# Sums of the first two column tiles shared by VectorE and TensorE, low parts ahead of shift and scale, earlier zeroing, and a new spread of the second layer's sums

## The chip, the cores and the metric

One core of a Trainium2 chip runs the whole program in one launch. The metric is the device time in microseconds (us), as the median of three runs. The names of the engines are those of the profile: PE is TensorE, DVE is VectorE, ACT is ScalarE, POOL is GpSimd, SP is SyncE, which only issues transfers here.

## The reference

256 tokens of width 1024 pass through two layers of a modulated block (retention, then a softmax attention with forget gates) and a second block (window attention, a gated linear recurrence and a feed-forward part). Everything is float32. What matters here is the start and the retention layer:

```python
c_act = jax.nn.silu(c)                                   # (1, 1024)
for i in range(DEPTH):                                   # DEPTH = 2
    shift, scale, gate = jnp.split(c_act @ mod_w[i] + mod_b[i], 3, axis=-1)   # mod_w[i]: 1024 x 3072
    h = _rms_norm(x, norm_g[i]) * (1.0 + scale[:, None, :]) + shift[:, None, :]
    y = _retention(h, ...)  if i == 0 else  _forgetting_attention(h, ...)
    x = x + gate[:, None, :] * y

# _retention: q, k, v, g = split(h @ w_in)  (1024 x 6144); rope on q, k; decayed scores; o = scores @ v
    o = _layer_norm(_from_chunks(o)).reshape(b, s, RET_DV)
    return (o.astype(h.dtype) * jax.nn.silu(g)) @ w_out  # w_out: 2048 x 1024
```

The product `c_act @ mod_w` is a vector by a matrix, so it costs the reading of the matrix (12 MB a layer) and little arithmetic on PE.

## The kernel before

**Products.** A product of float32 matrices is made of three products in a reduced format: each operand is split into a high part and a low part (`whi`, `wlo` for weights, `ahi`, `alo` for the left side), and PE adds high x high, high x low and low x high (L353 to L355 in `products`, L438 to L440 in `rows_unit`). Weights come in units of 512 KB (128 partitions x 1024 columns). For each unit SP issues the load into one of 8 raw buffers, ACT copies it to `whi` (L1754), DVE subtracts to get `wlo` (L995), and PE runs 12 products of 128x512. `ring_to(u)` on ACT and on DVE does this work for all items up to unit u. There are 3 buffers for the split parts, so ACT can split unit v only when PE has finished unit v-3.

**Item order.** `weight_stream` writes one list of items: weight units ("w") and "mod" items, each 128 rows of `mod_w` (1024 columns). SP loads them in list order, 8 in flight, and DVE works them off in list order, each raising the semaphore `used`. A mod item costs DVE one multiply-and-add of 128x1024 into `acc` (L1004 in the profile, a helper's line); it costs ACT and PE nothing.

**The first stage (units 0 to 11).** The normalised input is transposed per column tile k of 128 (`turn_x0`), then ACT applies shift and scale (`x0_high`) and makes the high part, DVE the low part (`x0_low`). Shift and scale of layer 0 are needed per column tile before anything can be multiplied: the columns of `mod_w[0]` for tiles (0), (1), (2,3), (4,5), (6,7), the groups g = 0 to 4, are loaded by SP between the first units (`load_mod`), 1 MB for each tile. DVE adds up rows 0 to 6 of eight, each weighted with a column of silu(c), into `macc` (`mod_sums`). PE multiplies row 7 directly and adds the sum over partitions of `macc` with a product of one column against ones (`shift_scale`, L421 and L423), DVE adds bias and gain (`modulated(k)`), ACT and DVE make the parts of the left side, and PE can run the units of this tile. Units 3j and 3j+1 belong to tiles 2j and 2j+1 (`rows_unit`), unit 3j+2 to both (`products`).

**Retention (units 12 to 47).** In each chunk of four units PE makes 512 columns of the projection. After each of the first four chunks DVE applies rope to two banks. From unit 28 on, `weigh(h)` computes a head, DVE takes mean and variance (`weighed`), normalises two 128x512 tiles from PSUM (L1001) and multiplies with silu(g) (`gated`). Layer 1's mod items and layer 0's gate items are spread over units 12 to 55. `after_ss` sums layer 1's `acc` over partitions on PE. Units 48 to 63 are the output projection.

**What sets the order.** Each engine's program is written out by hand in order of execution. Nothing is planned by a cost table, apart from the item list.

## Time and profile before

| | us |
|---|---|
| median of 3 runs | 745.84 (745.13 to 746.02) |
| the profiled execution | 745.61 |
| its span in the trace | 743.8 |
| PE busy | 712.3 (96%) |
| DVE busy | 508.4 (68%) |
| ACT busy | 379.3 (51%) |
| granted TensorE clock, mean | 0.986 of full |

The span runs from the first instruction to the last; 1.8 us of the execution lie around it. Busy shares are means over very different stages: over the first 16.7 us PE mostly waits, in most later stages it has no gap. A granted clock of 0.50 is the lower of TensorE's two levels (1.2 GHz), 1.00 the upper one (2.4 GHz). A float32 product appears twice in a row of the timeline ("x2" for one written instruction).

### The profile page before, as it was taken

How to read it: one execution, taken by the hardware profiler on the slowest of the kernel's cores; microseconds unless marked ns; L12 is line 12 of the kernel's file. 1: busy time of each engine (PE TensorE's matmuls, PEld its weight loads, DVE VectorE, ACT ScalarE, POOL GpSimd, SP SyncE). 2: the span in 40 equal slices, each digit the busy share in tenths (PEclk: the TensorE clock that was granted, in tenths of full speed). 3: DMA queues.
4: the chain of work that ended last, by engine and by line, in shares of the span. 5: the costliest groups of instructions: out<-in, count | busy, mean ns of one | idle time of the engine just before them, and what ended most of it. 6: DMA issues, size and time to landing. Idle time of an engine off the chain costs nothing.

```text
span 743.8 us, 9342 instructions
## 1 busy us (share of the span) xinstructions
PE 712.3 (96%) x3520; PEld 585.5 (79%) x3520; DVE 508.4 (68%) x731; ACT 379.3 (51%) x559; POOL 22.2 (3%) x36
## 2 busy tenths in 40 slices
PE   5899999999999899999999899999999999999996
PEld 4777777778778678878888788888887888888884
DVE  4787998796865867845577779966676465555444
ACT  5337543454544647663645664454566544444343
POOL 4100000000000000000001100000000000000000
PEclk8799999999999999999999999999999999999998
DMA  9997766657784357753245453343466556655511
GB/s 297 370 336 259 259 238 214 226 182 248 230 274 145 94 193 251 233 164 95 97 151 173 153 172 95 119 136 122 133 199 195 176 170 198 194 182 183 194 66 57
DMA packets 74476, 138.95 MB, mean 187 GB/s; under 512 B 5748, under 2 KB 18272, under 8 KB 74432
## 3 DMA queue, kind: packets, MB, share of 16 engines
q1 hardware_dynamic: 72816, 134.82, 55.4%
q0 software_dynamic: 880, 1.64, 0.7%
q10 hardware_dynamic: 736, 1.90, 0.7%
q8 instruction: 28, 0.46, 0.3%
q14 instruction: 16, 0.13, 0.1%
HBM read 137.30 MB, written 1.05 MB: 186 GB/s over the span
## 4 chain that ended last, share of the span: by engine, by line
PE 84%; DVE 9%; issue 3%; ACT 2%; DMA 1%; SPq 0%; DVEq 0%; ACTq 0%
PE G L353 22%; PE G L355 22%; PE G L354 22%; PE T L374 4%; DVE arena L995 2%; DVE wlo L995 2%; PE T L820 2%; PE T L693 1%; PE T L674 1%; PE G L438 1%; DMA arena<-in_mod_w_dram 1%; DVE arena L1004 1%; PE G L440 1%; PE G L439 1%; PE T L729 1%
## 5 line engine op out<-in xcount | busy, mean ns | idle before, releaser
L995 DVE TENSOR_TENSOR wlo<-raw,whi 128x1024 fp32r<-128x1024 f32 x206 | 251.2, 1223 | 137.9 <-ACT whi L1754 137.0
L353 PE MATMUL G<-whi,ahi 128*128 128x512 f32 x776 | 314.2, 405 | 6.0 <-DVE wlo L995 5.4
L355 PE MATMUL G<-whi,alo 128*128 128x512 f32 x776 | 303.9, 392 | 0.0
L354 PE MATMUL G<-wlo,ahi 128*128 128x512 f32 x776 | 303.2, 391 | 0.0
L1754 ACT ACTIVATE whi<-raw 128x1024 fp32r<-128x1024 f32 x206 | 217.2, 1059 | 131.2 <-PE G L355 118.1
L353 PEld LDWEIGHTS G<-whi,ahi 128*128 128x128 f32 x776 | 146.2, 188 | 38.8 <-DVE wlo L995 8.6
L355 PEld LDWEIGHTS G<-whi,alo 128*128 128x128 f32 x776 | 146.0, 188 | 31.8
L354 PEld LDWEIGHTS G<-wlo,ahi 128*128 128x128 f32 x776 | 146.4, 189 | 29.3 <-issue 1.4
L1756 ACT ACTIVATE arena<-T,st 128x128 f32<-128x128 f32 (+1 forms) x48 | 16.7, 422 | 39.8 <-DVE st L1372 39.8
L1754 ACT ACTIVATE ahi<-T 128x512 fp32r<-128x512 f32 x25 | 15.0, 599 | 42.3 <-PE T L374 42.3
L1756 ACT ACT_TABLE_LOAD x27 | 34.6, 1283 | 2.3 <-issue 1.8
L374 PE MATMUL T<-head,arena 128*128 128x128 f32 x212 | 32.5, 277 | 2.4 <-ACT arena L1756 0.9
L374 PEld LDWEIGHTS T<-head,arena 128*128 128x128 f32 x212 | 25.8, 144 | 9.1 <-ACT arena L1756 1.3
L995 DVE TENSOR_TENSOR alo<-T,ahi 128x512 fp32r<-128x512 f32 x25 | 17.3, 690 | 21.3 <-ACT ahi L1754 21.3
L1004 DVE SCALAR_TENSOR_TENSOR acc<-raw,cact,acc 128x1024 f32<-128x1024 f32 x24 | 30.7, 1281 | 1.6 <-DVE wlo L995 0.5
L995 DVE TENSOR_TENSOR arena<-arena 128x512 f32<-128x512 f32 (+7 forms) x46 | 23.0, 551 | 1.2 <-ACT arena L1756 0.9
L1004 DVE SCALAR_TENSOR_TENSOR arena<-arena,cact 128x512 f32<-128x512 f32 (+1 forms) x30 | 19.3, 645 | 1.0
L1756 ACT ACTIVATE st<-st 128x1 f32<-128x1 f32 (+3 forms) x21 | 4.3, 205 | 30.7 <-DVE st L999 18.8
L1372 DVE TENSOR_REDUCE st<-T 128x2 f32<-128x512 f32 (+1 forms) x18 | 12.3, 689 | 11.0 <-PE T L676 5.9
L438 PE MATMUL G<-whi,ahi 128*128 128x512 f32 x32 | 14.6, 455 | 5.2 <-DVE alo L995 3.1
L820 PEld LDWEIGHTS T<-arena 128*128 128x128 f32 x128 | 15.4, 191 | 0.9 <-DVE arena L995 0.4
L1754 ACT ACTIVATE arena<-T 128x512 f32<-128x512 f32 x11 | 6.5, 596 | 18.6 <-PE T L374 16.0
(212 smaller groups left out, 610.5 us busy)
## 6 DMA issues: line engine op xcount, KB each, us to landing
raw<-in_ret_w_in_dram SPq DMA_DIRECT2D x48, 512.0 KB, 5.3
raw<-in_w_gate_up_dram SPq DMA_DIRECT2D x40, 512.0 KB, 4.0
raw<-in_mod_w_dram SPq DMA_DIRECT2D x32, 512.0 KB, 5.2
raw<-in_fox_w_in_dram SPq DMA_DIRECT2D x32, 512.0 KB, 4.8
raw<-in_w_in_dram SPq DMA_DIRECT2D x28, 512.0 KB, 3.5
raw<-in_w_down_dram SPq DMA_DIRECT2D x22, 512.0 KB, 4.5
arena<-in_mod_w_dram SPq DMA_DIRECT2D x16, 512.0 KB, 8.7
raw<-in_ret_w_out_dram SPq DMA_DIRECT2D x16, 512.0 KB, 5.5
```

Source lines behind the costliest of these rows:

```text
L353: e.matmul(o, ah, wh, start=first and k == 0, stop=False)
L354: e.matmul(o, ah, wl, start=False, stop=False)
L355: done = e.matmul(o, al, wh, start=False, stop=last and k == 1)
L374: d = e.transpose(t[:, n * P:(n + 1) * P], s, idf)
L438: e.matmul(o, ah, wh, start=k == 0, stop=False)
L439: e.matmul(o, ah, wl, start=False, stop=False)
L820: d = e.matmul(t[:, h * P:(h + 1) * P], k[:, h, m * P:(m + 1) * P], q[:, h, m * P:(m + 1) * P], start=True, stop=True)
L995: e.tensor_tensor(o, a, b, op).then_inc(sig[name], 1)
L1004: e.scalar_tensor_tensor(out=o, in0=a, scalar=s, in1=b, op0=op0, op1=op1).then_inc(sig[name], 1)
L1372: e.tensor_reduce(st[:, 44 + 4 * r:44 + 4 * r + n], t[:, :].rearrange("p (h n) -> p h n", h=n), AX.X, ALU.max, negate=True).then_inc(sig[f ...
L1754: d = e.activation(o, a, f, scale=scale)
L1756: d = e.activation(o, a, f, scale=scale, bias=bias)
```

## The change

1. **Sums shared (groups 0 and 1).** `VECTOR_ROWS` gives DVE rows 0 to 3 for the first two groups and leaves rows 4 to 7 to PE (`own_rows`), which makes eight products of one column for a tile where it made two. The other groups stay at seven rows on DVE. The sums of tile 0 go to banks G, those of tile 1 to T[0] and T[1].
2. **Order on PE at the start.** 20 idle transposes instead of 24, then the own rows of tile 0, the transposes of the small rows and of both tiles (`turn_rows`), the rest of the sums, 6 idle transposes, the first half of unit 0 (columns 0 to 511), the sums of tile 1, the second half of unit 0.
3. **Low parts first.** In the first stage DVE makes `wlo` of unit 3j before `modulated` of its tiles; ACT splits one unit more before the left sides.
4. **Zeroing.** POOL clears `acc` (128x3072) right after its small row loads, where it waited for `used` >= 2.
5. **Table.** ACT no longer loads the square-root table ahead of the two squares.
6. **Angles.** The three pieces of the rope angles are made together behind `wlo` of unit 12.
7. **Retention.** The normalisation of a head moves from DVE to ACT (`normalise`: scale and bias from two columns), `gated` comes later.
8. **Spread of mod items.** The distances are given by a table; five items now come with units 12 to 15, fewer from unit 16 to 28, and again many from unit 44 on. `after_ss` moves from units 41 to 44 to units 52 to 55.

```diff
-    for j in range(24):
-        after.setdefault(j * 15 // 8, []).append(mods[j])
+    after = (-1, 0, 1, 2, 3, 6, 9, 13, 16, 18, 20, 23, 25, 27, 30, 32, 34, 35, 36, 38, 39, 40, 41, 42)
+VECTOR_ROWS = [4, 4, 7, 7, 7]
@@ PE
-            for _ in range(24):
-                e.transpose(G[2][:, 0:P], idf, idf)
+            keep_warm(20)
+            def own_rows(g, i, a):
+                r0 = VECTOR_ROWS[g]
+                for r in range(r0, 8):
+                    e.matmul(sums_of(SUMMED[g][i], a), mod_tile(g)[:, a, r, i * P:(i + 1) * P], cact[:, r:r + 1], start=r == r0, stop=False)
+            def other_rows(g, i, a):
+                on_.wait_ge(sig["macc"], g + 1)
+                return e.matmul(sums_of(SUMMED[g][i], a), macc[:, g % 2, a, i * P:(i + 1) * P], ones[:, 0:1], start=False, stop=True)
-            turn_x0(0)
-            shift_scale(0)
-            turn_x0(1)
-            rows_unit(0, 0)
-            shift_scale(1)
+            first_sums(0, turn_rows)
+            keep_warm(6)
+            rows_unit(0, 0, (0,))
             on_.wait_ge(sig["rows_read"], 3)
+            first_sums(1)
+            rows_unit(0, 0, (1,))
-                    if u + 2 in (43, 44, 45, 46):
-                        after_ss(u + 2 - 43)
+                if 4 <= n < 8:
+                    after_ss(n - 4)
@@ DVE
-            mod_sums(0, 0, 2)
             on_.wait_ge(sig["rms_act"], 1)
             e.reciprocal(st[:, 0:2], st[:, 0:2]).then_inc(sig["rms"], 1)
-            mod_sums(0, 2, 7)
+            mod_sums(0, 0, 4)
...
-            mod_sums(1, 0, 7)
...
+            mod_sums(1, 0, 4)
+            ring_to(1)
             modulated(1)
-            ring_to(1)
+            ring_to(2)
             x0_low(1)
             for g in (2, 3, 4):
                 k, u = 2 * g - 2, 3 * g - 3
                 mod_sums(g, 0, 4)
-                if g > 2:
-                    ring_to(u - 1)
+                ring_to(u - 1)
                 mod_sums(g, 4, 7)
+                ring_to(u)
                 modulated(k)
                 modulated(k + 1)
-                ring_to(u)
                 x0_low(k)
...
             u = 12
+            ring_to(u)
+            for part in range(3):
+                angles(part)
...
-                    on_.wait_ge(sig["left_turned"], 2 * h - 2)
-                    ts(on[:, h % 2, m, :], t[:, :], mv[:, 0:1], mv[:, 1:2], ALU.subtract, ALU.mult, "weigh_dve")
+                    stt(st[:, 2 + m:3 + m], mv[:, 0:1], -1.0, mv[:, 1:2], ALU.mult, ALU.mult, "weigh_dve")
-            chunk_of([[(weighed, 0), (gated, 0)], [], [], [(scored, 2)]])
-            chunk_of([[(scored, 3)], [(weighed, 1), (gated, 1)], [(left_low, 8)], [(left_low, 10)]])
+            chunk_of([[(weighed, 0)], [], [(gated, 0)], [(scored, 2)]])
+            chunk_of([[(scored, 3)], [(weighed, 1)], [(left_low, 8)], [(left_low, 10), (gated, 1)]])
@@ ACT
-            sqrt_table()
-            ring_to(1)
+            ring_to(2)
             x0_high(1)
-            ring_to(2)
-            ring_to(3)
-            x0_high(2)
-            x0_high(3)
-            ring_to(5)
-            for k in (4, 6):
+            for k in (2, 4, 6):
                 ring_to(3 * k // 2 + 1)
+            def normalise(h):
+                for m in range(2):
+                    on_.wait_ge(sig["weigh_dve"], 10 * h + 8 + 2 * m)
+                    on_.wait_ge(sig["left_turned"], 2 * h - 2)
+                    act(on[:, h % 2, m, :], T[bank_of["weigh", h, m]][:, :], ACT.Identity, "normed",
+                        scale=st[:, 21 + 2 * m:22 + 2 * m], bias=st[:, 2 + m:3 + m])
@@ POOL
+            fill(acc[:, :], 0.0, "acc_zero")
 ...
-            on_.wait_ge(sig["used"], 2)
-            fill(acc[:, :], 0.0, "acc_zero")
```

On PE, the start of the program before stands in a row as follows (`head` are the constants with the identity, `cact` is silu(c), `arena` holds the rows of `mod_w` and the normalised input; three rows make one sixth of the first unit's products):

```order
L383 MATMUL G<-head 128x128 x24
L387 MATMUL T<-head,rows 128x128
L374 MATMUL T<-head,arena 128x128 x2
L421 MATMUL T<-cact,arena 128x1
L423 MATMUL T<-ones,arena 128x1
L421 MATMUL T<-cact,arena 128x1
L423 MATMUL T<-ones,arena 128x1
L374 MATMUL T<-head,arena 128x128 x2
L438 MATMUL G<-whi,ahi 128x512
L439 MATMUL G<-wlo,ahi 128x512
L440 MATMUL G<-whi,alo 128x512
```

In the changed kernel, the same place on PE:

```order
L387 MATMUL G<-head 128x128 x20
L422 MATMUL G<-cact,arena 128x1 x8
L482 MATMUL T<-head,rows 128x128
L381 MATMUL T<-head,arena 128x128 x4
L427 MATMUL G<-ones,arena 128x1 x2
L387 MATMUL G<-head 128x128 x6
L471 MATMUL G<-whi,ahi 128x512
L472 MATMUL G<-wlo,ahi 128x512
L473 MATMUL G<-whi,alo 128x512
```

The products with `cact` grow from two to eight and stand ahead of the transposes; after one more triple like the last three rows, the eight and two products of tile 1 follow, where they stood behind all four triples.

On DVE, the second group of sums before, up to the low part of tile 2's left side (`AB` holds shift and scale):

```order
L999 TENSOR_SCALAR arena<-arena,cact 128x512
L1004 SCALAR_TENSOR_TENSOR arena<-arena,cact 128x512 x6
L995 TENSOR_TENSOR AB<-T,mbc 128x1
L1001 TENSOR_SCALAR AB<-T,mb,cols 128x1
L995 TENSOR_TENSOR AB<-T,mbc 128x1
L1001 TENSOR_SCALAR AB<-T,mb,cols 128x1
L995 TENSOR_TENSOR wlo<-raw,whi 128x1024
L995 TENSOR_TENSOR alo<-gate,ahi 128x256
```

The same place on DVE in the changed kernel:

```order
L1040 TENSOR_SCALAR arena<-arena,cact 128x512
L1045 SCALAR_TENSOR_TENSOR arena<-arena,cact 128x512 x6
L1036 TENSOR_TENSOR wlo<-raw,whi 128x1024
L1036 TENSOR_TENSOR AB<-T,mbc 128x1
L1042 TENSOR_SCALAR AB<-T,mb,cols 128x1
L1036 TENSOR_TENSOR AB<-T,mbc 128x1
L1042 TENSOR_SCALAR AB<-T,mb,cols 128x1
L1036 TENSOR_TENSOR alo<-gate,ahi 128x256
```

The low part of unit 3 has moved ahead of shift and scale; the same holds for units 6 and 9 in the next groups.

## Rows read from the trace of the kernel before

**Rows 1.** The page: busy time of the engines; `wlo` subtractions; mod items on DVE.
```profile
PE 712.3 (96%) x3520; PEld 585.5 (79%) x3520; DVE 508.4 (68%) x731; ACT 379.3 (51%) x559; POOL 22.2 (3%) x36
...
L995 DVE TENSOR_TENSOR wlo<-raw,whi 128x1024 fp32r<-128x1024 f32 x206 | 251.2, 1223 | 137.9 <-ACT whi L1754 137.0
...
L1004 DVE SCALAR_TENSOR_TENSOR acc<-raw,cact,acc 128x1024 f32<-128x1024 f32 x24 | 30.7, 1281 | 1.6 <-DVE wlo L995 0.5
```
**Rows 2.** Windows, PE: stretch, length, busy us (count), granted clock, DMA share, GB/s.
```profile
10.00:16.70 6.70, 2.87 (x14) 0.71 1.12 325
22.00:24.00 2.00, 0.04 (x1) 0.77 1.08 376
24.00:29.00 5.00, 5.00 (x12) 0.50 1.05 378
34.00:52.00 18.00, 16.53 (x81) 1.00 1.06 381
80.00:140.00 60.00, 56.46 (x261) 1.00 0.67 230
```
**Rows 3.** Timeline, 5 to 17 us: start, duration, instruction, [idle before <- releaser].
```profile
5.43 1.28 ACT L1756 ACT_TABLE_LOAD   x1
...
6.83 1.04 ACT L1752 ACTIVATE arena<-x 128x1024 f32<-128x1024 f32 x1
...
9.24 0.20 ACT L1756 ACTIVATE st<-st 128x2 f32<-128x2 f32 x1 [0.24 <-DVE st L1001]
9.65 0.35 DVE L999 TENSOR_SCALAR arena<-arena,cact 128x256 f32<-128x256 f32 x1 [0.44 <-DMA arena<-in_mod_w_dram]
...
10.55 2.57 DVE L1004 SCALAR_TENSOR_TENSOR arena<-arena,cact 128x256 f32<-128x256 f32 x5
...
11.11 0.30 PE L387 MATMUL T<-head,rows 128*128 128x128 f32 x1 [1.06 <-DMA rows<-in_fox_k_gain_dram]
...
13.18 0.58 PE L423 MATMUL T<-ones,arena 128*128 128x1 f32 x2 [0.60 <-DVE arena L1004]
...
14.05 0.57 PE L423 MATMUL T<-ones,arena 128*128 128x1 f32 x2
...
16.71 0.77 PE L438 MATMUL G<-whi,ahi 128*128 128x512 f32 x1 [1.57 <-DVE alo L995]
```
**Rows 4.** Timeline, 25 to 36 us: group 2's sums, unit 3's split, unit 3's start.
```profile
25.55 0.83 DVE L999 TENSOR_SCALAR arena<-arena,cact 128x512 f32<-128x512 f32 x1
...
26.08 1.06 ACT L1754 ACTIVATE whi<-raw 128x1024 fp32r<-128x1024 f32 x1 [1.77 <-DMA raw<-in_ret_w_in_dram]
...
26.42 4.76 DVE L1004 SCALAR_TENSOR_TENSOR arena<-arena,cact 128x512 f32<-128x512 f32 x6
...
31.52 0.36 PE L423 MATMUL T<-ones,arena 128*128 128x1 f32 x2
...
32.86 0.36 PE L423 MATMUL T<-ones,arena 128*128 128x1 f32 x2
...
35.22 0.47 PE L438 MATMUL G<-whi,ahi 128*128 128x512 f32 x1 [0.52 <-DVE alo L995]
```
**Rows 5.** Timeline, PE: first product of unit 6, last of unit 7, first of unit 9.
```profile
47.25 0.47 PE L438 MATMUL G<-whi,ahi 128*128 128x512 f32 x1 [0.50 <-DVE alo L995]
...
52.59 0.39 PE L440 MATMUL G<-whi,alo 128*128 128x512 f32 x1
...
58.48 0.47 PE L438 MATMUL G<-whi,ahi 128*128 128x512 f32 x1 [0.52 <-DVE alo L995]
```
**Rows 6.** Timeline, 73 to 133 us: angles, rope's wait, normalisation, a wait for `wlo`.
```profile
73.32 1.34 DVE L1004 SCALAR_TENSOR_TENSOR arena<-arena 128x256 f32<-128x256 f32 x3
...
81.37 0.66 PE L374 MATMUL T<-head,arena 128*128 128x128 f32 x4 [0.84 <-DVE arena L995]
...
126.94 0.81 DVE L1001 TENSOR_SCALAR arena<-T,st 128x512 f32<-128x512 f32 x1
...
132.25 0.50 PE L353 MATMUL G<-whi,ahi 128*128 128x512 f32 x1 [1.56 <-DVE wlo L995]
```

More of the change, by code:

```diff
@@ L116, in weight_stream @@
     mods = [mod(1, k, c0) for k in range(8) for c0 in (0, D)] + [mod(0, k, 2 * D) for k in range(8)]
-    after = {}
-    for j in range(24):
-        after.setdefault(j * 15 // 8, []).append(mods[j])
-    for n, u in enumerate(main):
-        out += [u, *after.get(n, [])]
+    after = (-1, 0, 1, 2, 3, 6, 9, 13, 16, 18, 20, 23, 25, 27, 30, 32, 34, 35, 36, 38, 39, 40, 41, 42)
+    for n in range(-1, len(main)):
+        if n >= 0:
+            out.append(main[n])
+        out += [mods[j] for j in range(24) if after[j] == n]
     fox = [u for c in range(8) for u in chunk(W1, 512 * c)]
@@ L375, in transposes, with keep_warm @@
                 d.then_inc(sig[name], 1)
+            def keep_warm(n):
+                for _ in range(n):
+                    e.transpose(G[2][:, 0:P], idf, idf)
             on_.wait_ge(sig["c_in"], 16)
@@ L417, in shift_scale, with summed, first_sums, rows_unit @@
                     on_.wait_ge(sig[f"mod_in{i}"], n)
+            def summed(k):
+                for m in range(2):
+                    ready[k, m] = (sig["x0"], k + 1)
+            def first_sums(g, between=None):
+                mod_landed(g)
+                for a in range(2):
+                    own_rows(g, 0, a)
+                if between is not None:
+                    between()
+                for a in range(2):
+                    d = other_rows(g, 0, a)
+                d.then_inc(sig["sums"], 1)
+                summed(g)
+            def shift_scale(g):
+                mod_landed(g)
                 for i, k in enumerate(SUMMED[g]):
                     for a in range(2):
-                        o = T[2 + k % 2][:, 256 + a:257 + a]
-                        e.matmul(o, raw0[:, a, 7, i * P:(i + 1) * P], cact[:, 7:8], start=True, stop=False)
-                        on_.wait_ge(sig["macc"], g + 1)
-                        d = e.matmul(o, sums[:, a, i * P:(i + 1) * P], ones[:, 0:1], start=False, stop=True)
+                        own_rows(g, i, a)
+                        d = other_rows(g, i, a)
                     d.then_inc(sig["sums"], 1)
-                    for m in range(2):
-                        ready[k, m] = (sig["x0"], k + 1)
-            def rows_unit(u, k):
+                    summed(k)
+            def rows_unit(u, k, columns=(0, 1)):
                 on_.wait_ge(sig["used"], item_of[u] + 1)
@@ L432, in rows_unit @@
                 j = u % NH
-                for c in range(2):
+                for c in columns:
                     wh, wl = whi[:, j, c * 512:(c + 1) * 512], wlo[:, j, c * 512:(c + 1) * 512]
@@ L443, in rows_unit, with turn_rows @@
                     done_at[u, c] = products_n[0]
-            turn_x0(0)
-            shift_scale(0)
-            turn_x0(1)
-            rows_unit(0, 0)
-            shift_scale(1)
+            def turn_rows():
+                on_.wait_ge(sig["filled"], 1)
+                on_.wait_ge(sig["rows_in"], 16 * 9)
+                t = bank("rows", sig["rows_read"], 3)
+                e.transpose(t[:, 0:P], rows[:, :], idf).then_inc(sig["rows_turned"], 1)
+                turn_x0(0)
+                turn_x0(1)
+            first_sums(0, turn_rows)
+            keep_warm(6)
+            rows_unit(0, 0, (0,))
             on_.wait_ge(sig["rows_read"], 3)
+            first_sums(1)
+            rows_unit(0, 0, (1,))
             for k in range(0, 8, 2):
@@ L1187, in _ @@
                     u += 1
-                    if c == 0 and k < 3:
-                        angles(k)
-                    elif c == 3 and k >= 2:
+                    if c == 3 and k >= 2:
                         scored(k - 2)
@@ L1240, in chunk_of @@
                 for k in range(4):
-                    if u + 2 == 46:
-                        after_ss()
                     ring_to(u + 2)
@@ L1272, in _ @@
             for n in range(12):
+                if n == 8:
+                    after_ss()
                 ring_to(u + 2)
```

44 lines of the change are left out of this document (20 added, 24 removed).

## The prediction

> **What bounds the kernel now.** I read the page first. PE is busy for 712.3 of 743.8 us [rows 1], so no work is to be saved: the change has to fill gaps of PE, or to keep its clock up. The table of windows says where they lie [rows 2]. From 10 to 16.7 us PE is busy for 2.87 of 6.70 us, and the granted clock sinks to 0.71 in the mean. From 22 to 24 PE stands still, and from 24 to 29 it runs at 0.50, the lower level, where twelve products take the whole 5 us. From 34 to 52 it lacks 1.5 us, with the clock at 1.00. From 80 to 140 it lacks 60.00 - 56.46 = 3.5 us. One more thing is in these rows: up to 52 us the DMA share stays above 1 and 325 to 381 GB/s flow, so in the first stage transfers land when they land, whatever the engines do.
>
> The timeline then shows each gap's last wait. At the start the chain runs through DVE's seven rows of group 0, the sums on PE, shift and scale, ACT and the low part, and unit 0 starts at 16.71 [rows 3]. Unit 3 starts at 35.22 behind the low part of its left side; unit 6 at 47.25 and unit 9 at 58.48 likewise [rows 4, 5]. In retention PE waits for rope (0.84 at 81.37) and once 1.56 for a `wlo` that stands on DVE behind normalisation, gate and a mod item [rows 6].
>
> **The start.** Group 0 lands at 9.65 in both kernels [rows 3]. Five additions took 2.57, 0.51 each, so four rows end at 9.65 + 0.35 + 3 x 0.51 = 11.5 on DVE, where seven ended at 13.18. PE's new products: at full clock six steps of this kind take 32.86 - 31.52 = 1.34, 0.22 each [rows 4]; at the lower one two take 14.05 - 13.18, 0.44 each [rows 3]. Eight own products from 9.65 end at 11.4 (13.2 at the lower clock). The small rows come at 11.11 and are not moved. One transpose of 0.30, four short ones (0.6 together), two products of 0.22: the sums of tile 0 are there at about 12.8, before at 14.05 + 0.44 = 14.5. Behind them runs the same chain, 16.71 - 14.5 = 2.2. Unit 0 starts at 15.0, 1.7 earlier. The six idle transposes lie in this chain's wait.
>
> Dropping the early table load costs nothing on this path: the load of 1.28 at 5.43 stood ahead of the first square (6.83); now the two squares, 1.04 each, come first and the load follows at about 7.6. The root is then possible at about 9, at 9.24 before [rows 3]. For this price there is a rule that speaks against the change. In rows 3 a square follows the load's end within 0.12 us, and the load starts at 5.43, at the end of the instruction before. The Trainium skill (ScalarE: Activation LUTs, What ACT_TABLE_LOAD costs) adds a drain of about 1.4 us to each load; by it the root would come 1.4 later and unit 0 up to as much, at 16.4 instead of 15.0. The trace does not bear the drain out.
>
> Zeroing `acc` earlier takes POOL out of DVE's way: one scaling of 128x512 took 0.83 at 25.55 [rows 4]. Half of that at most is won, and it isn't late there any more. The other end is a loss of as much if POOL's small loads came later; nothing waits for those in this stage. I take 0.
>
> **Units 0 to 2 and the start of unit 3.** From 15.0: six products of 0.23 (52.59 - 47.25 = 5.34 for 23 steps [rows 5]) to 16.4, ten short ones of tile 1 to 18.6 (19.4 if their rows or the first half come later), six products to 20.9, and unit 1 from about 21.8, where shift, scale and the low part of unit 2 (1.22 [rows 1]) stand ahead of it. Before, it came behind 23 us and ran at the lower clock. If the clock is low for part of this, some six to ten products at +0.2 each, unit 1 ends between 24.5 and 26. Four transposes and half of unit 2 add 2.0, the eight sums of group 2 add 1.8: they end at 28.3 to 29.8.
>
> Here the moved low part counts. Unit 3's raw data land at 26.08, ACT needs 1.06 [rows 4] and DVE 1.22, so shift and scale of tile 2 cannot be made before 28.4. Behind them stand 2.1 for AB, ACT and the low part (the chain above). Unit 3 starts at 30.6, at 35.22 before: **4.6 gained**. Faster work upstream gives no more; this landing is the floor. Before, the same low part stood behind shift and scale and delayed the left side's.
>
> **Groups 3 and 4.** 36 products of 0.232 are 8.35, four transposes 0.6, eight sums 1.8: 10.75 of work for PE. Before, a group took 47.25 - 35.22 = 12.0 and then 58.48 - 47.25 = 11.2. With `wlo` out of the chain sums, shift and scale, left side, 0.3 of waiting remains, and I take 11.0: unit 9 at 52.6 instead of 58.48, **1.3 more, 5.9 together**. The landings allow it: unit 6's data are 3.7 MB behind unit 3's, 9.6 us at 381 GB/s, so at 35.7, and are wanted at about 38.
>
> **Units 12 to 15.** Unit 12 starts at 52.6 + 8.35 = 61.0. On DVE `wlo` of unit 12 ends at about 58.0; behind it now stand three pieces of angles (1.34 for one [rows 6], 4.0), a mod item (1.28 [rows 1]) and `wlo` of unit 13 (1.22): 64.5. PE wants it at 61.0 + 2.8 = 63.8. **0.7 lost.** From then on each unit brings 1.28 + 1.22 = 2.5 on DVE against 2.8 on PE. The five items are the price paid for fewer later.
>
> **Units 16 to 47.** Rope then starts when PE is done with its banks, not 1.5 later; in each chunk DVE loses a mod item of 1.28 or two, and in the stretch of 132.25 two normalisations (0.81 each) for two tiny instructions, and the two products with the gate step back behind two `wlo`. All 3.5 of idle time should go but for 0.2 in each of two chunks, where one mod item still stands between rope and `wlo`: **3.1 gained**. The normalisation costs ACT something the trace doesn't show in this form; between 0.2 (its two-column root [rows 3]) and 1.06 (a full split), and I take 0.8, DVE's for the same tile. ACT is busy for 51% and sits behind PE's buffers; were it on the path, eight of them would cost 6.4.
>
> **Late items and the rest.** From unit 44 to 55 nearly every unit has a mod item: 2.5 against 2.8, with buffers for two units as cover; 0 taken. `after_ss` is the same 16 products of 0.22 at another place: 0.
>
> **Sum.** 5.9 - 0.7 + 3.1 = 8.3. The profiled execution took 745.6 (span 743.8 and 1.8 around it), 0.2 under the median of the runs. Forecast: 745.6 - 8.3 = **737.3 us**.
>
> **The rivals.**
> *The clock stays down through units 0 to 2.* It fell in the stretch of 10 to 16.7 and again after 22 [rows 2], both times behind short products and a wait; the new start has twenty one-column products, ten of them between the halves of unit 0. The Trainium skill (TensorE: Matmul & The Clock Gate, Part 1) says the lower clock is the default and activity lifts it; the rows agree. For it to last, the six idle transposes would have to be too few. Then the ten short ones take 4.4, unit 1 ends at 29, and unit 3 starts at 34.2: 1.0 gained instead of 4.6, **740.9**.
> *DVE becomes the bound where items are dense.* Units 12 to 15 ask it for four `wlo`, five items and the angles, 4.9 + 6.4 + 4.0 = 15.3, against 11.1 on PE. If its lead is used up by then, 4.2 are lost instead of 0.7: **740.8**. For it: DVE is full from 80 on before. Against it: it waited 137.9 us for `whi`, so it usually has a lead [rows 1].
> *The low parts tie each group to its landing.* If units 6 and 9 land 2 later than I count, unit 9 starts 2 later: **739.3**. Against it: 381 GB/s is a mean of 18 us.
> *Slower: the clock is low as far as unit 5.* A product takes 0.42 then (5.00 for 12 [rows 2]), 0.2 more. Before, about 18 ran so; now it would be 72 of six units, 54 x 0.2 = 10.8 more, against the 8.3 gained: **748**. It decides from 42 more such products on (8.3 / 0.2). Between 34 and 52 PE stood still for 1.5 in sum and kept 1.00 [rows 2], which speaks against it.
> *The change doesn't do what it says*: DVE's additions weren't the last wait at the start but the small rows at 11.11; then 0.5 of the 1.7 goes, hidden by the floor at 26.08 anyway.
>
> **How the numbers follow.** The forecast, 0.62, with a range of its own of 735.3 to 739.3; clock 0.13; dense items 0.12; landings 0.07; slower 0.05, the rest (0.01) near no change. Range for 8 in 10: 735.0 to 741.5, which takes in the clock's and the items' cases and leaves out the slower one and a gain of over 10. A measurement of this kernel tells 0.2% (1.5 us) from no change. Faster 0.92, same 0.03, slower 0.05.
>
> **What would show it.** Unit 0's first product near 15.0, unit 3's near 30.6 behind a `whi` released by its raw data near 26.1; unit 9 near 52.6; granted clock 1.00 from 24 to 29; a wait for `wlo` under 1 us near 64; PE idle under 0.6 in the 60 us from unit 16 on; no wait at unit 31. The forecast is wrong if unit 3 starts after 32, if the clock shows 0.50 beyond 24, or if PE waits for `wlo` more than 2 us in units 12 to 16.

## Result and profile after

| us | before | after |
|---|---|---|
| median | 745.49 (744.32 to 746.02, 6 runs) | 739.07 (735.23 to 741.07, 6 runs) |
| profiled execution | 745.61 | 737.51 |
| its span | 743.8 | 735.7 |
| granted clock, mean | 0.986 | 0.997 |

The ratio is 0.9912, 95% interval 0.9884 to 0.994. The medians are 6.4 us apart, the two profiled executions 8.1. The changed kernel scatters by 5.8 us where the kernel before scatters by 1.7. That scatter turns out to be the main thing to explain.

The page of the changed kernel, the row of the engines, beside [rows 1]:

```profile
PE 712.5 (97%) x3546; PEld 587.4 (80%) x3546; DVE 502.0 (68%) x725; ACT 384.1 (52%) x566; POOL 22.1 (3%) x36
```

PE's work is what it was (712.5 against 712.3). What went is its idle time. The windows of PE after the change (stretch, length, busy us and count, granted clock, DMA share, GB/s) answer to [rows 2]:

```profile
10.00:16.70 6.70, 6.68 (x31) 1.00 1.12 320
16.70:20.00 3.30, 2.60 (x6) 1.00 1.08 352
24.00:29.00 5.00, 4.40 (x22) 1.00 1.06 381
34.00:52.00 18.00, 18.00 (x98) 1.00 1.06 381
80.00:140.00 60.00, 59.46 (x272) 1.00 0.63 211
```

From 34 to 52 no idle time is left, and from 80 to 140 it is 0.54, where 3.54 stood. From 24 to 29 there are 22 products, where twelve ran at 0.50. The first two rows deceive, though. They say 1.00, but PE is busy for 6.68 of 6.70 us and unit 0 still starts late. The timeline of the start shows why (start, duration, instruction, idle before and releaser), beside [rows 3]:

```profile
5.24 4.53 PE L387 MATMUL G<-head 128*128 128x128 f32 x20
...
5.97 2.68 POOL L2297 MEMSET acc<- 128x3072 f32 x1
...
7.61 1.28 ACT L1794 ACT_TABLE_LOAD   x1
7.62 1.05 DVE L1042 TENSOR_SCALAR st<-st 128x2 f32<-128x2 f32 x1 [7.62 <-ACT arena L1790]
...
8.90 0.20 ACT L1794 ACTIVATE st<-st 128x2 f32<-128x2 f32 x1
...
9.94 3.55 PE L422 MATMUL G<-cact,arena 128*128 128x1 f32 x16 [0.18 <-DMA arena<-in_mod_w_dram]
...
10.38 1.53 DVE L1045 SCALAR_TENSOR_TENSOR arena<-arena,cact 128x256 f32<-128x256 f32 x3
...
15.16 1.52 PE L387 MATMUL G<-head 128*128 128x128 f32 x6
...
17.40 0.77 PE L471 MATMUL G<-whi,ahi 128*128 128x512 f32 x1 [0.72 <-DVE alo L1036]
17.96 0.63 PE L472 MATMUL G<-wlo,ahi 128*128 128x512 f32 x1
18.39 0.63 PE L473 MATMUL G<-whi,alo 128*128 128x512 f32 x1
...
20.10 2.28 PE L422 MATMUL T<-cact,arena 128*128 128x1 f32 x16
```

Eight own products (16 entries) take 3.55 us, 0.44 each, and the six idle transposes 1.52, 0.25 each. The six products of unit 0 stand 0.43 apart, as the twelve at a granted 0.50 did (5.00 / 12 = 0.42, [rows 2]). So PE ran at the lower level from its start to about 21 us, whatever the windows say. The trace's own record of the clock begins only at 21.0 us, with the upper level, and a window counts time without a record as 1.00. DVE had its four rows done at 11.9; PE was the late one. From 20.10 the eight own products of tile 1 take only 2.28: within them the clock rises.

The starts of the units, each from its first product in the timelines, give the ledger of the whole gain:

| first product of | before | after | gained so far | forecast |
|---|---|---|---|---|
| unit 0 | 16.71 | 17.40 | -0.7 | +1.7 |
| unit 3 | 35.22 | 33.08 | 2.1 | 4.6 |
| unit 9 | 58.48 | 54.19 | 4.3 | 5.9 |
| unit 12 | 66.77 | 62.43 | 4.3 | 5.9 |
| unit 16 | 77.65 | 74.53 | 3.1 | 5.2 |
| unit 30 | 127.25 | 122.45 | 4.8 | |
| unit 31 | 132.25 | 125.65 | 6.6 | 8.3 |
| unit 100 | 397.53 | 391.10 | 6.4 | 8.3 |
| unit 110 | 430.76 | 422.73 | 8.0 | 8.3 |
| end | 743.8 | 735.7 | 8.1 | 8.3 |

The last step of 1.6 lies far from anything the change touches. In the kernel before PE waits twice for the residual there (timeline):

```profile
413.12 0.66 PE L374 MATMUL T<-head,x 128*128 128x128 f32 x4 [0.69 <-DVE x L995]
...
415.02 0.66 PE L374 MATMUL T<-head,x 128*128 128x128 f32 x4 [1.24 <-DVE x L995]
```

A window of PE in the same trace shows the clock lower behind them:

```profile
416.00:420.00 4.00, 4.00 (x13) 0.62 0.42 131
```

In the changed kernel the same two waits stand there (0.69 and 1.23 us), and the clock stayed up. Over the fourteen profiles of this study (both kernels and twelve variants) the stretch from unit 100 to unit 110 takes either 31.6 us (ten of them) or 33.2 (before, e3, e7, e12); the one from unit 110 to the end takes 312.9 to 313.1 in all. So 1.6 us of the profiled gain is this fall of the clock, which comes behind the same waits in some executions and not in others. Without it the gain is 6.4 in the profile, as it is between the medians.

### The profile page after: what moved, and what is told of

It reads as the page before. It is cut to its first block, busy times and chain, and to the rows that moved or that the text cites. A ratio compares the mean times of both kernels' runs of the same rounds, so it can differ in the third digit from the quotient of the medians.

```text
span 735.7 us, 9394 instructions
## 1 busy us (share of the span) xinstructions
PE 712.5 (97%) x3546; PEld 587.4 (80%) x3546; DVE 502.0 (68%) x725; ACT 384.1 (52%) x566; POOL 22.1 (3%) x36
## 3 DMA queue, kind: packets, MB, share of 16 engines
HBM read 137.30 MB, written 1.05 MB: 188 GB/s over the span
## 4 chain that ended last, share of the span: by engine, by line
PE 88%; DVE 7%; ACT 2%; issue 2%; DMA 1%; SPq 0%; DVEq 0%; ACTq 0%
PE G L360 23%; PE G L362 22%; PE G L361 22%; PE T L381 4%; PE T L861 2%; DVE wlo L1036 2%; PE T L734 1%; PE T L715 1%; DVE arena L1036 1%; DMA arena<-in_mod_w_dram 1%; DVE arena L1045 1%; PE G L471 1%; PE G L472 1%; PE G L473 1%; PE T L770 1%
## 5 line engine op out<-in xcount | busy, mean ns | idle before, releaser
L360 PE MATMUL G<-whi,ahi 128*128 128x512 f32 x776 | 314.0, 405 | 4.7 <-DVE wlo L1036 4.2
L1794 ACT ACTIVATE arena<-T,st 128x128 f32<-128x128 f32 (+2 forms) x56 | 22.4, 471 | 39.8 <-DVE st L1410 39.8
L1410 DVE TENSOR_REDUCE st<-T 128x2 f32<-128x512 f32 (+1 forms) x18 | 12.3, 689 | 11.0 <-PE T L717 5.9
L1045 DVE SCALAR_TENSOR_TENSOR arena<-arena,cact 128x512 f32<-128x512 f32 (+1 forms) x24 | 16.4, 685 | 0.9
L1792 ACT ACTIVATE arena<-arena 128x512 f32<-128x512 f32 x14 | 8.3, 639 | 14.4 <-DVE arena L1036 14.4
L861 PE MATMUL T<-arena 128*128 128x128 f32 x128 | 15.7, 275 | 0.0
```

Source lines behind the costliest of these rows:

```text
L360: e.matmul(o, ah, wh, start=first and k == 0, stop=False)
L861: d = e.matmul(t[:, h * P:(h + 1) * P], k[:, h, m * P:(m + 1) * P], q[:, h, m * P:(m + 1) * P], start=True, stop=True)
L1045: e.scalar_tensor_tensor(out=o, in0=a, scalar=s, in1=b, op0=op0, op1=op1).then_inc(sig[name], 1)
L1410: e.tensor_reduce(st[:, 44 + 4 * r:44 + 4 * r + n], t[:, :].rearrange("p (h n) -> p h n", h=n), AX.X, ALU.max, negate=True).then_inc(sig[f ...
L1792: d = e.activation(o, a, f, scale=scale)
L1794: d = e.activation(o, a, f, scale=scale, bias=bias)
```

## Experiments

Unless something else is said, each kernel is the changed one with the edit shown; "u3" is the start of unit 3's first product. Three groups ran (e1 to e4, e5 to e8, e9 to e12), each beside its own 11 runs of the kernel before, with medians 745.94, 745.17 and 745.37. The 95% interval of every variant's ratio overlaps that of the changed kernel (0.9884 to 0.994), so the medians alone separate none of them from it. What an edit does is read from the distances in the profiled executions, one for each kernel.

### e1: all seven rows of every group on DVE

```diff
-VECTOR_ROWS = [4, 4, 7, 7, 7]
+VECTOR_ROWS = [7, 7, 7, 7, 7]
-            mod_sums(0, 0, 4)
+            mod_sums(0, 0, 7)
-            mod_sums(1, 0, 4)
+            mod_sums(1, 0, 7)
```

> The changed kernel with one thing undone: DVE adds up seven rows again in groups 0 and 1 too, PE multiplies only row 7 itself; the order on PE stays. Theory A (sharing the sums takes work off the chain, as predicted): the sums of tile 0 come later, macc at about 13.5 instead of 11.9, unit 0 starts about 1 later than the 17.4 of the changed kernel, unit 3 0.5 to 1 later, time +0.5 to +1. Theory B (the own products run at the lower clock, 3.55 us for eight, so they are the last wait at the start themselves and sharing gives nothing): unit 0 starts at 16.4 to 17.2, unit 3 within 0.5 of 33.1, time within 0.5 of the changed kernel's 739.

Measured 736.61 (735.54 to 738.55, 5 runs), ratio 0.9891 [0.9874, 0.9908]; u0 16.64, u3 31.86, u31 124.17. PE in the timeline of e1:

```profile
9.91 0.98 PE L422 MATMUL G<-cact,arena 128*128 128x1 f32 x4 [0.15 <-DMA arena<-in_mod_w_dram]
...
13.53 1.01 PE L427 MATMUL G<-ones,arena 128*128 128x1 f32 x4 [1.47 <-DVE arena L1045]
...
16.64 0.76 PE L471 MATMUL G<-whi,ahi 128*128 128x512 f32 x1 [0.72 <-DVE alo L1036]
```

The clock is at its lower level here too (0.98 for two products; the record begins at 24.5 us), but PE has only two of them and waits 1.47 us for DVE. Unit 0 starts 0.8 earlier than with shared sums, as theory B had it, and unit 3 1.2 earlier, which neither theory had. The sharing, meant to shorten the start, lengthened it in the profiled execution of the changed kernel.

### e2: low parts of units 3, 6 and 9 behind shift and scale again

```diff
-                ring_to(u)
                 modulated(k)
                 modulated(k + 1)
+                ring_to(u)
```

> The changed kernel with one thing undone: the low part of units 3, 6 and 9 stands behind shift and scale again. If the moved low parts give what the prediction said, each of the three starts is 0.4 to 0.8 later: unit 9 at 55.5 to 56.5 instead of 54.19, time +1.5 to +2. If the landing of the raw data binds there (rival), units 3, 6 and 9 start as before or earlier: +0.

Measured 740.79 (739.36 to 741.81, 6 runs), ratio 0.9937 [0.9923, 0.9951]. Unit 0 started at 15.02 in this execution, so only the distances tell: unit 3 to unit 6 and unit 6 to unit 9 take 11.24 and 11.23, against 10.56 and 10.55 with the low parts first. PE waits again in each group:

```profile
45.47 0.48 PE L471 MATMUL G<-whi,ahi 128*128 128x512 f32 x1 [0.48 <-DVE alo L1036]
...
56.70 0.48 PE L471 MATMUL G<-whi,ahi 128*128 128x512 f32 x1 [0.48 <-DVE alo L1036]
```

The order is worth 0.7 us in each of groups 3 and 4. If it is worth as much in group 2, which this execution can't show, that makes about 2, near the 1.7 between the medians.

### e3: mod items spread evenly, as before

```diff
-    after = (-1, 0, 1, 2, 3, 6, 9, 13, 16, 18, ...)
+    after = (0, 1, 3, 5, 7, 9, 11, 13, 15, 16, ...)
```

> The changed kernel with the old distances of the mod items (none ahead of unit 12, every second unit). Theory: the waits in units 16 to 31 come back in part, +1.7 at units 17 and 18 and up to +0.5 at unit 31, while the 1.2 lost at units 13 and 14 is won back: net +0.5 to +1.5. Rival (the normalisation alone removed the waits): net -1.2.

Measured 739.88 (738.02 to 740.28, 5 runs), ratio 0.992 [0.9906, 0.9934]. From unit 12 to unit 31 this kernel takes 63.88 us, the changed one 63.22, the one before 65.48. One wait is back in retention, at unit 18:

```profile
81.89 0.50 PE L360 MATMUL G<-whi,ahi 128*128 128x512 f32 x1 [0.59 <-DVE wlo L1036]
```

The spread is worth 0.7 us, inside the theory's range, but of the 1.2 lost in units 12 to 15 only 0.2 comes back (unit 12 to unit 16 takes 11.91 us here, 12.10 in the changed kernel, 10.88 before). Most of the gain in retention is not the spread's doing, nor is most of that loss.

### e4 and e10: 26 idle transposes at the start instead of 20

```diff
-            keep_warm(20)
+            keep_warm(26)
```

> The changed kernel with 26 idle transposes at the start instead of 20. Theory (clock): the transposes of the changed kernel stand 0.22 apart, which is the lower level, and PE's clock rises only at about 20 us; with six more the clock has risen before the own products, which then take 1.8 instead of 3.55: unit 0 at 15.5 to 16.3 instead of 17.4, unit 3 about 1 earlier, time -0.5 to -1.5, and less scatter between runs. Rival (the six stand in the way): the own products start 0.5 to 1 later, at the same low rate, and everything is that much later, time +0.5 to +1.

Measured 735.39 (734.82 to 738.08, 4 runs), ratio 0.9873 [0.9855, 0.989]. PE in the timeline of e4:

```profile
9.90 1.92 PE L422 MATMUL G<-cact,arena 128*128 128x1 f32 x16 [0.26 <-DMA arena<-in_mod_w_dram]
...
12.62 0.85 PE L387 MATMUL G<-head 128*128 128x128 f32 x6
14.86 0.76 PE L471 MATMUL G<-whi,ahi 128*128 128x512 f32 x1 [1.39 <-DVE alo L1036]
```

The theory's cause came, with more effect than it expected (15.5 at best for unit 0). The own products take 1.92 instead of 3.55. Unit 0 starts at 14.86 (forecast 15.0), unit 3 at 30.44 (30.6), unit 9 at 51.74 (52.6). What binds unit 3 here are DVE's own items one behind the other: the last sum of group 2 ends at 27.33 and `wlo`, released by nothing, runs from 27.25. The raw data were there at 25.35:

```profile
25.01 2.33 DVE L1045 SCALAR_TENSOR_TENSOR arena<-arena,cact 128x512 f32<-128x512 f32 x3
25.35 1.06 ACT L1792 ACTIVATE whi<-raw 128x1024 fp32r<-128x1024 f32 x1 [3.67 <-DMA raw<-in_ret_w_in_dram]
...
27.25 1.22 DVE L1036 TENSOR_TENSOR wlo<-raw,whi 128x1024 fp32r<-128x1024 f32 x1
```

The same kernel ran a second time, as e10:

> The changed kernel with 26 idle transposes instead of 20, a second time, on another chip job: is it a version that beats both kernels by more than its own scatter? Theory (the six transposes bridge the wait for group 0, so that the own products run at the upper level): 735.4, between 734.8 and 738.1, unit 0 at about 14.9 and unit 3 at about 30.4. Rival (four runs happened to fall well; the clock's moment is luck whatever the count): a median near the changed kernel's, 738 to 739, with a scatter of 4 us or more, and unit 0 at 15.6 or later.

Measured 735.72 (735.35 to 739.79, 5 runs), ratio 0.9884 [0.9865, 0.9903]; u0 14.65, u3 31.18. Seven of the nine runs of e4 and e10 lie below 737, of the six of the changed kernel one. By its medians it is the fastest version of the study, about 10 us below the kernel before. Against the changed kernel the intervals still overlap, and e11 (735.94) and e1 (736.61) can't be told from it.

### e5: normalisation on DVE again, everything else as changed

```diff
+                    ts(on[:, h % 2, m, :], T[bank_of["weigh", h, m]][:, :], mv[:, 0:1], mv[:, 1:2], ALU.subtract, ALU.mult, "normed")
...
-                    act(on[:, h % 2, m, :], T[bank_of["weigh", h, m]][:, :], ACT.Identity, "normed",
-                        scale=st[:, 21 + 2 * m:22 + 2 * m], bias=st[:, 2 + m:3 + m])
```

> The changed kernel with the normalisation of the heads back on DVE (two scalings of 128x512 a head, 0.81 each, beside the tiny instructions; gated stays in its later place). Theory of the prediction: the wait of unit 31 (1.56 before, gone after) was removed by taking 1.6 of work off DVE and by the later gate; undone, 0 to 0.6 of it comes back, because the gate (1.28) still stands behind: time +0 to +0.6. Rival (the ACT version is what counts): the whole 1.8 between units 30 and 31 comes back. Rival (it costs ACT, and ACT was on the path): time falls by up to 0.8 elsewhere in units 28 to 47.

Measured 739.23 (737.8 to 739.51, 4 runs), ratio 0.9916 [0.9903, 0.993]. From unit 30 to unit 31 it takes 3.92 us, against 3.20 in the changed kernel and 5.00 before. DVE and PE in its timeline, from the second of the two normalisations on:

```profile
121.61 0.80 DVE L1042 TENSOR_SCALAR arena<-T,st 128x512 f32<-128x512 f32 x1
122.33 1.27 DVE L1045 SCALAR_TENSOR_TENSOR acc<-raw,cact,acc 128x1024 f32<-128x1024 f32 x1
123.53 2.35 DVE L1036 TENSOR_TENSOR wlo<-raw,whi 128x1024 fp32r<-128x1024 f32 x2
124.79 0.50 PE L360 MATMUL G<-whi,ahi 128*128 128x512 f32 x1 [0.48 <-DVE wlo L1036]
```

Of the 1.8 us gained there, 0.7 come from moving the normalisation, 1.1 from the rest. That rest is the later gate or the spread; e3, with the old spread, takes 3.20 here too, which points to the gate. A second price shows later: between units 47 and 49, where nearly every unit has a mod item, e5 falls back by another 0.9 against the changed kernel (6.68 us from unit 47 to 49, 182.06 to 188.74, where that takes 5.80; 1.1 by unit 100), and PE waits for the last gate there:

```profile
188.32 0.66 PE L381 MATMUL T<-head,arena 128*128 128x128 f32 x4 [0.53 <-DVE arena L1036]
```

So the late items are free only because the normalisation is gone from DVE: the move of the normalisation is worth 0.7 + 1.1 = 1.8 us. The medians (739.23 against 739.07) don't show it: unit 3 started 1.4 earlier in e5's profiled execution, which hides as much. On ACT it costs PE nothing: no wait for it stands in the changed kernel's trace.

### e6: the three pieces of the angles apart, one in each of units 13 to 15

```diff
-            for part in range(3):
-                angles(part)
...
+                    if c == 0 and k < 3:
+                        angles(k)
```

> The changed kernel with the three pieces of the rope angles between units 12 to 15 again instead of all behind unit 12's wlo. Theory: the 1.2 lost ahead of units 13 and 14 come from these 4 us on DVE; split, the wlo of unit 13 ends about 2.4 earlier: 1.0 to 1.2 is won back at unit 13, perhaps 0.3 lost at units 15 or 16, time -0.7 to -1.2. Rival (the mod items ahead of units 12 and 13 are what delays it): unit 13 still waits 0.5 or more.

Measured 738.31 (736.97 to 741.49, 6 runs), ratio 0.9917 [0.9899, 0.9935]. Unit 13 follows unit 12 by 2.72, without the wait. But the waits come back at unit 16 and before rope's transposes:

```profile
72.46 0.50 PE L360 MATMUL G<-whi,ahi 128*128 128x512 f32 x1 [0.42 <-DVE wlo L1036]
76.79 0.66 PE L381 MATMUL T<-head,arena 128*128 128x128 f32 x4 [1.27 <-DVE arena L1036]
```

Unit 12 to unit 18 takes 19.40 us, against 18.60 with the angles together: 0.8 worse. Up to unit 16 the split wins 0.6 (11.46 against 12.10), from there to unit 31 it loses 1.5 (52.63 against 51.12). The median lies 0.8 below the changed kernel's, as the theory had it, but the distances don't bear its reason out: in the profiled execution unit 0 had started 1.8 earlier. DVE has to make the angles before rope in any case, and late is worse than together.

### e7: seven rows on DVE and 26 idle transposes

The edits of e1 and e4 in one kernel.

> The changed kernel with 26 idle transposes and seven rows on DVE: is sharing worth something once the clock is up? If sharing works as the prediction had it at the full clock: unit 0 about 1.0 to 1.5 later than the 14.86 of the same kernel with shared sums, unit 3 within 0.5 to 1 of its 30.44, time +0.5 to +1 against that kernel's 735.4. If not: within 0.4 of it.

Measured 737.78 (737.71 to 738.38, 4 runs), ratio 0.9903 [0.9889, 0.9917]; u0 16.23, u3 31.96, u31 124.21. Two rows of its PE timeline, beside those of e1:

```profile
9.93 0.58 PE L422 MATMUL G<-cact,arena 128*128 128x1 f32 x4 [0.26 <-DMA arena<-in_mod_w_dram]
...
13.52 0.61 PE L427 MATMUL G<-ones,arena 128*128 128x1 f32 x4 [2.06 <-DVE arena L1045]
```

The clock is up (0.58 for what took 0.98), and PE only waits longer for DVE. With the four profiles e1, e7, e4 and the changed kernel the sharing has two prices. At the upper level it wins 1.4 us at unit 0, 1.5 at unit 3 and 1.2 at unit 31 (e7 less e4). At the lower one it loses 0.8, 1.2 and 1.5 (the changed kernel less e1). These are differences of single executions, whose clocks differ behind unit 0 too (low until 25.3 us in e7, until 18.3 in e4), so only the price at unit 0 is the sharing's alone. The medians of e4 and e7 are 2.4 apart, but e7's profile holds the 1.6 of units 100 to 110 and e4's doesn't.

### e8 and e12: more idle transposes in the second place too

e8 has 26 and 16 of them and the angles of e6, e12 has 26 and 12.

```diff
-            keep_warm(20)
+            keep_warm(26)
-            keep_warm(6)
+            keep_warm(16)
```

> The changed kernel with 26 idle transposes at the start, 16 instead of 6 between the sums and unit 0, and the angles split again. Theory: the start as with 26 (2.6 earlier), unit 0's products at 0.23 instead of 0.43 because PE does not stand still before them (up to 1.2 earlier at unit 1, mostly hidden by unit 3's floor, which is the raw data at 26.1), and 1.0 from the angles: 734 to 735. Rival: the ten more transposes end after the left side is ready and delay unit 0 by up to 0.5, and the clock is up anyway: no gain over 26 alone but the 1.0 of the angles.

> 26 idle transposes at the start and 12 instead of 6 behind the sums of tile 0, where PE waited for 1.39 us for the low part with the six in place. Theory: the six more fill 0.7 to 0.9 us of that wait at the upper level, delay nothing, and the clock cannot fall before unit 0; the median is that of 26 alone, 735 to 736, with less scatter. Rival (they are still running when the low part is ready, or the clock is low and they take 0.2 us each instead of 0.14): unit 0 starts 0.3 to 1 us later and the median is 0.5 to 1 us above 26 alone.

e8 measured 736.88 (735.87 to 740.72, 6 runs), ratio 0.9902 [0.988, 0.9924]; u0 16.04, u3 31.03. e12 measured 737.8 (736.91 to 738.41, 4 runs), ratio 0.9895 [0.9881, 0.9909]; u0 15.92, u3 32.56. PE in the timeline of e12:

```profile
10.29 1.92 PE L422 MATMUL G<-cact,arena 128*128 128x1 f32 x16 [0.20 <-DMA arena<-in_mod_w_dram]
...
13.64 2.52 PE L387 MATMUL G<-head 128*128 128x128 f32 x12
15.92 0.48 PE L471 MATMUL G<-whi,ahi 128*128 128x512 f32 x1
```

And the low part of the left side on DVE, in e12 and then in e4:

```profile
15.30 0.43 DVE L1036 TENSOR_TENSOR alo<-gate,ahi 128x256 fp32r<-128x256 f32 x1
...
14.29 0.42 DVE L1036 TENSOR_TENSOR alo<-gate,ahi 128x256 fp32r<-128x256 f32 x1
```

In e4 unit 0 starts 0.15 behind the end of this low part, in e12 0.19. So the twelve idle transposes cost at most 0.04, although no wait of PE stands ahead of unit 0 any more. They took 2.52, where 0.85 for six is the upper level's price, so most of them ran at the lower level, but they ran beside a low part that was 1.0 late itself. Of that, 0.4 is group 0, which landed later than in e4, and 0.6 the clock, which was low from 12.3 us (in e4 from 14.9): the transposes and sums of tile 0 took longer. By unit 2 e12 is ahead of e4 by 0.5 (24.98 against 25.45), since unit 0's products stand 0.23 apart. It loses 2.1 again at unit 3, where DVE waits 1.28 for the data of group 2 and six products ahead of the unit stand 0.43 apart. The rival of e12 has the number (unit 0 1.1 later, median 2.1 to 2.4 above 26 alone) without its reason.

In e8 the idle transposes do stand in the way: its low part ends at 15.35 and unit 0 starts 0.7 behind it, so the sixteen cost some 0.5, as its rival had it. Its theory (734 to 735) failed in this and in the angles, which cost instead of winning (e6).

### e9: 26 idle transposes, `acc` cleared late, as before

```diff
             fill(gains[:, :], 1.0, "filled")
-            fill(acc[:, :], 0.0, "acc_zero")
...
+            on_.wait_ge(sig["used"], 2)
+            fill(acc[:, :], 0.0, "acc_zero")
```

> The changed kernel with 26 idle transposes at the start (735.39 us in an earlier run), and the zeroing of acc moved back behind used >= 2, where it stood before the change. My theory (the prediction's: the zeroing only takes POOL out of the way of one scaling): the scaling of 128x512 at about 24 us is stretched again from 0.48 to about 0.83 us, unit 3 starts at most 0.4 us later, and the median is the same as with 26 transposes alone, within 0.5 us. Rival: POOL's small loads, which now wait behind the clearing, come earlier and unit 0 starts earlier by 0.3 us or more; then the median falls. The short scaling of 128x2 at 7.6 us should take 0.2 instead of 1.05 us in either case and move nothing, since the table load covers it.

Measured 737.55 (735.63 to 740.52, 6 runs), ratio 0.99 [0.9877, 0.9924]. In its timeline DVE and POOL show both effects that were expected:

```profile
7.64 0.17 DVE L1042 TENSOR_SCALAR st<-st 128x2 f32<-128x2 f32 x1 [7.64 <-ACT arena L1790]
...
19.16 2.66 POOL L2297 MEMSET acc<- 128x3072 f32 x1 [10.58 <-DVE wlo L1036]
...
21.09 1.00 DVE L1040 TENSOR_SCALAR arena<-arena,cact 128x512 f32<-128x512 f32 x1 [0.17 <-DMA arena<-in_mod_w_dram]
```

The small scaling is short again, the large one takes 1.00, and neither moves the end: the profiled executions of e9 and e10 are 735.63 and 735.70, unit 12 at 60.74 and 60.78. The zeroing is worth nothing. The median is 1.8 above e10's since three of six runs lie at 739.3 to 740.5 and three at 735.6 to 735.8. One of e10's five lies up there too, so this is not shown to be the edit's doing.

### e11: 32 idle transposes

> The changed kernel with 32 idle transposes. Six more than 26, so they end at about 10.2 to 10.5 us (26 took 4.40 us from 5.24), behind the landing of group 0 at 9.6 to 9.9. Theory (the clock has to be up before the own products): those start up to 0.6 us later, but always at the upper level: unit 0 between 14.9 and 15.5, unit 3 at 30.4 to 31, a median of 735 to 736.5 and the smallest scatter of all. Rival (more idle work only delays, the clock's moment depends on something else): unit 0 at 16 or later in spite of them, median 737 to 739, scatter as with 20.

Measured 735.94 (734.87 to 740.53, 6 runs), ratio 0.9886 [0.9863, 0.9909]; u0 16.06, u3 31.19. PE in its timeline:

```profile
5.14 6.19 PE L387 MATMUL G<-head 128*128 128x128 f32 x32
11.17 1.84 PE L422 MATMUL G<-cact,arena 128*128 128x1 f32 x16
```

They ended at 11.3, not at 10.5, and the own products started at 11.17 without a wait ahead of them, 1.3 later than in e4. So unit 0 came at 16.06, as the rival had it, and the median inside the theory's range. The own products ran at the upper level, but the scatter (5.7 us) is as large as the changed kernel's. More than 26 brings nothing more, and neither number makes every execution good.

## Why the prediction was right in sum and wrong in a term

**The start failed.** The step "Unit 0 starts at 15.0" priced eight own products at 0.22, ending at 11.4, and noted 13.2 for the lower clock. It was the second: they took 3.55 and ended at 13.5, behind DVE. The rest of the chain ran at the lower level too, and unit 0 came at 17.40, 0.7 later than before instead of 1.7 earlier. At its core this is the rival "the clock stays down through units 0 to 2", which had 0.13. It was down earlier than that rival had it, and up again at about 21 us, where the rival let it stay down through unit 2. e4 shows that the rest of the step was sound: with the clock up, unit 0 starts at 14.86 and unit 3 at 30.44.

**Unit 3 and its floor.** Expected were 4.6 gained behind a floor at 26.08 + 1.06 + 1.22 = 28.4. The landing was as counted; the timeline of the changed kernel, to be read beside [rows 4]:

```profile
25.20 4.76 DVE L1045 SCALAR_TENSOR_TENSOR arena<-arena,cact 128x512 f32<-128x512 f32 x6
...
26.13 1.06 ACT L1792 ACTIVATE whi<-raw 128x1024 fp32r<-128x1024 f32 x1 [1.82 <-DMA raw<-in_ret_w_in_dram]
...
29.88 1.22 DVE L1036 TENSOR_TENSOR wlo<-raw,whi 128x1024 fp32r<-128x1024 f32 x1
31.01 0.15 DVE L1036 TENSOR_TENSOR AB<-T,mbc 128x1 f32<-128x1 f32 x1
...
33.08 0.46 PE L471 MATMUL G<-whi,ahi 128*128 128x512 f32 x1
```

But DVE began the six sums of group 2 at 25.20, since it had made the left side of unit 1 just before, which was to be ready by 21.8 and came at 24.8. `wlo` stood behind these sums until 29.88. The forecast had counted landing, ACT and `wlo` alone; DVE's own queue of 4.8 us ahead of `wlo` was not in the floor. The last 2.1 (31.01 to 33.08) are the chain that the prediction carried over. Gained: 2.1. By the prediction's own mark ("wrong if unit 3 starts after 32") this step is wrong, in the profiled execution. In e1 and e4 to e11 unit 3 starts between 30.4 and 32.0.

**Groups 3 and 4** were mis-sized the other way: 10.56 and 10.55 each instead of 11.0. The 0.3 of waiting left in the sum was not there, and PE's work in a group was 10.55, where 10.75 was counted. They gained 2.2 instead of 1.3. e2 attributes 1.4 of that to the low parts. The landings held nothing up.

**Units 12 to 15** lost 1.2 instead of 0.7. The cause was named rightly; the timeline of the changed kernel:

```profile
63.73 1.27 DVE L1045 SCALAR_TENSOR_TENSOR acc<-raw,cact,acc 128x1024 f32<-128x1024 f32 x1
64.92 1.21 DVE L1036 TENSOR_TENSOR wlo<-raw,whi 128x1024 fp32r<-128x1024 f32 x1
66.19 0.50 PE L360 MATMUL G<-whi,ahi 128*128 128x512 f32 x1 [0.88 <-DVE wlo L1036]
```

The angles (59.56 to 63.8), one item and `wlo` of unit 13 stand in a row, 6.6 us in all, as counted. (That the angles fit is partly luck: the row of 1.34 is one of their three pieces, the pieces are unequal, and together they take 4.2 us where 3 x 1.34 was counted.) DVE's lead was 0.2 less (2.8 from the end of `wlo` of unit 12 at 59.64 to that unit's start, 3.0 in the forecast), and PE gave 0.3 more behind the wait: unit 13 started 3.76 behind unit 12, 1.0 more than before, for a wait of 0.88, and unit 14 lost 0.2 again. The rival of DVE as the bound, with 4.2 lost, did not come.

**Units 16 to 47** gained 3.5 instead of 3.1: 1.7 by unit 18, 1.8 at unit 31, where no wait is left. Undone one at a time from unit 16 to 31, the angles give back 1.5 (e6), the spread 0.9 (e3) and the normalisation 0.7 (e5, and 1.1 beyond that as cover for the late items). These overlap in units 16 to 18, where the angles alone give back 1.4 and the spread 0.8 of the 1.7. The later gate was not undone by itself; what e5 leaves of the gain at unit 31, 1.1, is put down to it by elimination. With the angles late, e6 took 19.40 from unit 12 to 18, the kernel before 19.05 (66.77 to 85.82). **Late items, `after_ss`, zeroing, table:** taken as 0; from unit 31 to unit 100 the ledger moves by 0.2, and e9 confirms the zeroing. In between it is misleading: unit 47 comes 10.3 us earlier than before and unit 56 6.5, because `after_ss` left units 41 to 44 for 52 to 55. The table load cost no path time: the root runs at 8.90, directly behind the load that ends at 8.89, and 9.24 was its time before; no run undid this edit by itself.

**Sum.** 2.1 + 2.2 - 1.2 + 3.5 - 0.2 = 6.4 by unit 100, and 1.6 from the clock between units 100 and 110 makes 8.0, 8.1 at the end. So the 737.5 of the profiled execution, against 737.3, is a hit by two errors that cancel: 2.5 too much at unit 3, 2.2 too little in the rest (5.9 measured, 3.7 forecast, 1.6 of the difference by the clock at units 100 to 110). The median of 739.07 is the fairer figure, inside the range, at the upper end of the forecast's own, and as far from the 737.3 of the forecast as from the 740.9 of the clock's rival. "Slower" and "doesn't do what it says" did not come.

## What to carry to other kernels

Moving work to TensorE at the start of a kernel is worth what its clock is at that moment: at the first unit it won 1.4 us here with the upper level and lost 0.8 with the lower one, in one profiled execution each, and the same instructions met both. Price such a step at both levels, and cut idle work that keeps the engine busy last, not first: with 26 or 32 idle transposes (e4, e9, e10, e11) 14 of 21 executions lie below 737 us, with 20 in the changed kernel one of six. Where an engine works in a fixed order, what another engine needs for later (`wlo`) can stand in the shadow of what it waits for now; that gave the steadiest gain, 0.7 us in each of two groups. A wait that stems from work with a deadline, like the angles, moves when it is split; it goes only if the work can be done earlier.

## What the runs showed of the hardware

**The granted clock can be listed as 1.00 while PE runs at the lower level.** The record of the clock in a trace need not begin with the kernel, and a window counts time without a record as 1.00. In the changed kernel the record begins at 21.0 us, in e1 at 24.5, in the other twelve profiles at 8.0 to 10.4, each time with the upper level. In the window from 10 to 16.7 us of the changed kernel it reads 1.00, and the own products take 0.44 us each; from 17.4 to 20 likewise, products 0.43 apart. The distance of equal products is the surer sign. The means of the whole span (0.997, 0.998 in e1) are therefore too high.

**The moment of the rise is not fixed by the program.** The changed kernel, e2, e3, e5 and e6 have the same instructions as far as unit 0, and in their profiled executions it starts at 17.40, 15.02, 14.84, 15.58 and 15.62. The 26 transposes alone took 4.40, 4.53, 4.57, 4.71, 4.82 and 5.59 us in e4, e7, e9, e10, e12 and e8, in the order in which their records begin (8.0, 8.2, 8.4, 8.6, 8.9 and 10.4). In the changed kernel PE was busy from 5.24 to 16.7 with no gap above 0.2 us, and the clock rose only at 21.0. What decides the moment stays open. From unit 31 on the profiles differ only by the 1.6 at units 100 to 110, but for the 1.1 of e5. No execution between 738.5 and 741 us of the changed kernel itself, of e4 or of e9 to e11 was profiled. The mean clocks on record say what the slow ones have in common: of the 21 executions of e4, e9, e10 and e11 the 14 below 737 us have 0.992 to 0.997, the seven above 738 have 0.986 to 0.988. The difference of the means, 0.008 of some 736 us, is by estimate 11 us more at a granted 0.50, for 4.0 us more time. Where in the program these lie, and why, stays open.

**A short VectorE instruction can be held by a memset on GpSimd.** The scaling of 128x2 took 1.05 us in the changed kernel, from 7.62 to 8.67, and the memset ran from 5.97 to 8.65; with the memset elsewhere it took 0.17 (e9). The scaling of 128x512 took 0.48 without and 0.83 to 1.00 with a memset beside it. The Trainium skill (SBUF — State Buffer, Who interferes with whom) says that the two engines share a pair of ports which, in VectorE's two-port modes, one of them holds for a whole instruction while the other is blocked. The traces agree in that each scaling ends just behind its memset: the small one 0.02 us behind, those of 128x512 0.28 (before) and 0.27 (e9).

**A table load without a drain.** The load ran from 7.61 to 8.89 and the root began at 8.90. The Trainium skill (ScalarE: Activation LUTs, What ACT_TABLE_LOAD costs) adds about 1.4 us of drain to each switch to another table set. Here nothing of it stands behind the load, and ahead of it there are 0.02 us (7.59 to 7.61).
